# Hybrid pooling and gating layer on Trainium2: the first chunk's seven first weight units advance together, one block of h at a time

## The reference, cut to what matters

```python
mod = jax.nn.silu(c) @ w_ada + b_ada
shift, scale, gate = jnp.split(mod, 3, axis=-1)
h = _layer_norm(x) * (1 + scale[:, None]) + shift[:, None]
proj = h @ w_in                                  # 1024 -> 5 x 512
xa, ga, u, v, gb = jnp.split(proj, SPLITS, axis=-1)
ya = _pool_mixer(xa, w_pool, pool_scale) * jax.nn.silu(ga)
yb = _sgu_mixer(gelu(u), gelu(v), sgu_ln_g, sgu_ln_b, w_sgu, b_sgu) * jax.nn.silu(gb)
y = jnp.concatenate([ya, yb], axis=-1) @ w_out
z = DEEPNORM_ALPHA * x + gate[:, None] * y
return _layer_norm(z) * ln_g + ln_b
```

## Time and profile before

| | |
|---|---|
| median of 3 runs | 708.24 us (707.89 to 710.29) |
| span of the profiled execution | 708.7 us |
| TensorE busy | 684.2 us (97%), 3141 matmuls |
| VectorE busy | 531.2 us (75%) |
| ScalarE busy | 258.0 us (36%) |
| GpSimd busy | 108.3 us (15%) |
| HBM read | 89.94 MB |

### The profile page before, as it was taken

The page is one execution under the profiler, slowest core; times in us unless marked ns, Lnnn a source line. Parts: engine busy times, 40 slices in busy tenths (PEclk is TensorE's granted clock), DMA queues, the critical chain, the costliest instruction groups (busy, mean ns, idle before and its releaser), DMA issues.

```text
span 708.7 us, 8888 instructions
## 1 busy us (share of the span) xinstructions
PE 684.2 (97%) x3141; PEld 569.3 (80%) x3141; DVE 531.2 (75%) x942; ACT 258.0 (36%) x344; POOL 108.3 (15%) x96
## 2 busy tenths in 40 slices
PE   8789999899999999999999999999999999999993
PEld 8668888778888888888888888888888888888882
DVE  5876778995559979886468988886476997656387
ACT  4426435436412343334521243334621344332201
POOL 2461115520002201000002210110001210000005
PEclk9689999999999999999999999999999999999997
DMA  8933574216232561334233453234222532225203
GB/s 343 344 130 118 181 291 154 90 59 238 90 114 95 177 231 68 118 115 154 90 119 111 140 211 131 89 119 178 89 96 83 178 121 101 100 79 220 95 1 118
DMA packets 28362, 98.81 MB, mean 139 GB/s; under 512 B 3074, under 2 KB 4130, under 8 KB 28324
## 3 DMA queue, kind: packets, MB, share of 16 engines
q1 hardware_dynamic: 28324, 98.34, 39.2%
HBM read 89.94 MB, written 8.39 MB: 139 GB/s over the span
## 4 chain that ended last, share of the span: by engine, by line
PE 81%; DVE 13%; POOL 2%; issue 2%; ACT 1%; DMA 1%; SPq 0%; DVEq 0%; ACTq 0%; POOLq 0%
PE bank_b L852 51%; PE bank_a L852 25%; DVE v_gelu L571 4%; PE bank_b L876 2%; PE bank_a L945 1%; DVE w_low L533 1%; DMA x_norm<-in_x 1%; POOL gate_rows L359 1%; PE bank_b L902 1%; DVE sum_b L652 1%; DVE x_stats L552 1%; DVE z L732 1%; DVE z_stats L734 1%; DVE x_norm L558 1%; DVE tanh L729 1%
## 5 line engine op out<-in xcount | busy, mean ns | idle before, releaser
L852 PE MATMUL bank_b<-h_high,w_high 128*128 128x512 f32 x512 | 201.0, 393 | 0.0
L852 PE MATMUL bank_b<-h_high,w_low 128*128 128x512 f32 x512 | 199.4, 389 | 0.0
L852 PE MATMUL bank_b<-h_low,w_high 128*128 128x512 f32 x512 | 199.3, 389 | 0.0
L533 DVE TENSOR_TENSOR w_low<-w_float,w_high 128x1024 fp32r<-128x1024 f32 x108 | 137.0, 1269 | 48.6 <-ACT w_high L415 48.6
L415 ACT ACTIVATE w_high<-w_float 128x1024 fp32r<-128x1024 f32 x112 | 118.3, 1057 | 135.2 <-PE bank_a L852 61.0
L852 PEld LDWEIGHTS bank_b<-h_high,w_low 128*128 128x128 f32 x512 | 96.1, 188 | 20.3
L852 PEld LDWEIGHTS bank_b<-h_high,w_high 128*128 128x128 f32 x512 | 96.1, 188 | 19.9 <-issue 0.2
L852 PEld LDWEIGHTS bank_b<-h_low,w_high 128*128 128x128 f32 x512 | 96.2, 188 | 19.8 <-issue 0.2
L322 POOL TENSOR_TENSOR z_rstd<-z_var_eps,minus_half 128x1 f32<-128x1 f32 x16 | 21.6, 1351 | 359.9 <-DVE z_var_eps L737 359.9
L852 PE MATMUL bank_a<-w_high,h_high 128*128 128x512 f32 x128 | 52.7, 412 | 0.0
L852 PE MATMUL bank_a<-w_low,h_high 128*128 128x512 f32 x128 | 51.8, 405 | 0.0
(11 more groups left out here) (142 smaller groups left out, 975.7 us busy)
## 6 DMA issues: line engine op xcount, KB each, us to landing
w_float<-in_w_units SPq DMA_DIRECT2D x112, 512.0 KB, 3.3
z<-in_mod_units SPq DMA_DIRECT2D x20, 512.0 KB, 6.3
x_norm<-in_x SPq DMA_DIRECT2D x16, 512.0 KB, 5.3
z<-in_x SPq DMA_DIRECT2D x16, 512.0 KB, 4.2
out<-z SPq DMA_DIRECT2D x14, 512.0 KB, 4.7
ln_g_rows<-in_mod_units SPq DMA_DIRECT2D x2, 512.0 KB, 8.4
ln_b_rows<-in_mod_units SPq DMA_DIRECT2D x2, 512.0 KB, 8.8
out<-z SPq DMA_DIRECT2D x4, 256.0 KB, 2.0
```

What stands on the lines that cost most here:

```text
L533: vec.tensor_tensor(wL[:, n % S_SLOTS, :], wF[:, n % F_SLOTS, :], wH[:, n % S_SLOTS, :].bitcast(F32), ALU.subtract).then_inc(w_low, 1)
L852: last = mm(bank, wl if n == 2 else wh, ml if n == 1 else mh, start=start and n == 0, stop=stop and n == 2)
```

## The change

It touches the first chunk only, but for three added waits.

- SyncE loads all four x tiles first, and then eight weight units in the order EARLY = (0, 4, 5, 6, 1, 2, 3, 7), each after two mods.
- A mod of the first four serves one block of h instead of two (the host packs them so). TensorE multiplies mods 0 to 4 itself, VectorE adds up the other 11.
- Whole x tiles are turned (eight transposes each) into two banks, and ScalarE (tiles 0 and 1) and VectorE (tiles 2 and 3) copy the turned, normalised x back over its tile in x_norm. `h_evacuate` reads it from there. The last x tile is normalised by VectorE. The short warm-ups after the first 22 are gone.
- TensorE takes each block k of h through the v unit, unit 4 and unit 5, and, after each second block, unit 6. These use A, B0, B1 and B2; B3 keeps the shift and scale columns.
- GpSimd makes no subtraction any more; it computes the offsets of x. VectorE makes all low halves. Unit 6 borrows the buffers v_high and v_low.
- The parts of the gating matrix and its bias are prepared before the gelu of v in ScalarE's program, and pool and gating products come after units 8 and 9 instead of 7 and 8, and 11 instead of 10.

```diff
+POOL_AFTER_FIRST = (8, 11, 14, 18)
+SGU_AFTER_FIRST = (9, 11, 14, 18)
+EARLY = (0, 4, 5, 6, 1, 2, 3, 7)
+EARLY_CHANNEL = (4, 5, 6)
-PE_MODS = (0, 1)
+PE_MODS = (0, 1, 2, 3, 4)
-WARM_UP = (22, 1, 3, 0, 4)
+WARM_UP = 22
...
+            for p, unit in enumerate(EARLY):
+                for m in range(2 * p, 2 * p + 2):
+                    load_m(m)
+                load_w(0, p, unit)
...
                 if isinstance(c, int) and c == 0:
+                    act.wait_ge(staged_act, 2)
+                    act.wait_ge(staged_dve, 2)
+                    act.wait_ge(mod_ready, (1, 2)[k] if k < 2 else 2 + k // 2)
...
+                    nc.scalar.activation(hH[:, k, :].rearrange("p (j t) -> p j t", j=TILES), staged(k), ACT.Identity,
+                                         bias=shift, scale=scale).then_inc(h_high, 1)
...
+            small_weights()
+            sgu_bias()
+
             def chunk(c, first, last):
...
+                            wait(act, gb_gated, c * G + g)
                             nc.scalar.activation(tanh[:, :], B[:, 1, :], ACT.Tanh, scale=0.5).then_inc(ga_tanh, 1)
...
-                    if (n + AHEAD < UNITS or not last) and not (first and n + AHEAD < V_UNITS):
+                    if (n + AHEAD < UNITS or not last) and not (first and n + AHEAD < len(EARLY)):
                         split_low(c, n + AHEAD)
...
+            x_norm_of(0, TILES - 1, x0_last)
+            x_stage(2, B[:, 0:2, :])
+            mod_cols_of(0)
+            x_stage(3, A[:, 0:2, :])
+            split_low(0, 0, EARLY[0])
+            h_split(0, 0)
+            split_low(0, 1, EARLY[1])
+            split_low(0, 2, EARLY[2])
+            mod_cols_of(1)
+            mod_sum(5)
+            h_split(0, 1)
...
+            warm(WARM_UP)
+            turn_tile(0, A[:, 0:2, :])
+            turn_tile(1, A[:, 2:4, :])
+            mod_own_tile(0)
+            turn_tile(2, B[:, 0:2, :])
+            mod_own_tile(1)
+            pe.wait_ge(staged_act, 1)
+            turn_tile(3, A[:, 0:2, :])
+            pe.wait_ge(mod_ready, 1)
+            mod_own_tile(2)
...
+            for k in range(KT):
+                q = k // 2
+                pe.wait_ge(h_high, k + 1)
+                pe.wait_ge(w_low, EARLY.index(q) + 1)
+                early_v(k, (0, 1))
+                if k == 0:
+                    mod_own_tile(3)
+                pe.wait_ge(h_low, k + 1)
+                done = early_v(k, (2,))
+                if k % 2 == 1:
+                    done.then_inc(unit_done, 1)
+                if k == 1:
+                    pe.wait_ge(mod_ready, 2)
+                    mod_own(4)
+                if k == KT - 2:
+                    turn_w_sgu()
+                if k < KT - 1:
+                    early_channel(4, (k,))
+                    early_channel(5, (k,))
+                    if k % 2 == 1:
+                        early_channel(6, (k - 1, k))
+                        if q < V_UNITS - 1:
+                            mod_columns(q + 1)
+                else:
+                    sgu_bias()
+                    early_channel(4, (k,)).then_inc(unit_done, 1)
+                    early_channel(5, (k,)).then_inc(unit_done, 1)
+                    early_channel(6, (k - 1, k)).then_inc(unit_done, 1)
```

More of the change, by code:

```diff
@@ L205, in run_chunks, with after, w_slot, staged @@
             chunk(CHUNKS - 1, False, True)
+        def after(first):
+            return (POOL_AFTER_FIRST, SGU_AFTER_FIRST) if first else (POOL_AFTER, SGU_AFTER)
+        def w_slot(c, n):
+            early = isinstance(c, int) and c == 0 and n in EARLY
+            s = EARLY_SLOT[n] if early else n % S_SLOTS
+            if s == SPARE_SLOT:
+                return tuple(t[:, 0:2, :].rearrange("p a b -> p (a b)") for t in (vH, vL))
+            return wH[:, s, :], wL[:, s, :]
+        def staged(k):
+            return xn[:, :, k * P:(k + 1) * P]
         def m_sem(m):
@@ L752, in chunk @@
                     x_steps.begin(c + 1)
-                for n in range(UNITS):
-                    if (n + AHEAD < UNITS or not last) and not (first and n + AHEAD < V_UNITS):
+                if first:
+                    small_weights()
+                pool_after, sgu_after = after(first)
+                for n in range(V_UNITS if first else 0, UNITS):
+                    if (n + AHEAD < UNITS or not last) and not (first and n + AHEAD < len(EARLY)):
                         split_low(c, n + AHEAD)
@@ L773, in chunk @@
                             pooled_low(c, g)
+                            wait(dve, yp_ready, c * G + g)
                             gate(ga_tanh, ga_gated, sga, 1, c * G + g + 1)
@@ L889, in mod_own, with mod_own_tile @@
+            def mod_own_tile(m):
                 pe.wait_ge(c_ready, 1)
                 m_wait(pe, m)
-                for k in (2 * m, 2 * m + 1):
+                k_out = m // 2
+                for a in range(4):
+                    k = 4 * (m % 2) + a
+                    for i in range(2):
+                        col, at = a * 2 * P + i * P, 2 * i + k_out
+                        last = mm(B[:, 3, at:at + 1], m_slot(m)[:, col:col + P], csilu[:, k:k + 1],
+                                  start=(m % 2 == 0 and a == 0 and i == 0), stop=(m % 2 == 1 and a == 3),
+                                  skip_group_check=True)
+                last.then_inc(mod_multiplied, 1)
```

344 lines of the change are left out of this document (182 added, 162 removed).

## The result

The changed kernel takes **730.63 us** (median of 4 runs, 729.92 to 731.21), against 708.86 us for the kernel before (4 runs, 707.89 to 710.29) in the same session: a ratio of **1.031, interval 1.028 to 1.033**. It is slower, as forecast, but by some 22 us, where the forecast was 5.6 on the span. 730.6 lies outside the range of 707.6 to 720.2.

The account below looks back on a forecast made before the run. TensorE was taken to bound the seven first units, then VectorE the pooling: 90.6 + 9.4 + 0.75 + 61.8 = 162.6 against 156.97, so 708.7 + 5.6 = 714.3 span, median 713.8. Range 707.6 to 720.2.

Parts of the forecast that it names:

- The start: Up to block 1: first product about 19.9 us, half clock to about 28.6, block 1 at 31.4.
- From block 1 to the last v product: Seven-unit block on TensorE: products, sums, transposes and three waits of 1.0 take 39.3 us, ending at 70.7.
- rival 2: Clock keeps falling: two stretches at the start give +8.7 us, one more fall within the block +12; chance 0.22.
- From V to pooling 1: After the last v product: unit 8 starts 19.9 us later, TensorE stands 8.4, pooling of group 1 follows after 9.4.
- From pooling 1 on: VectorE sets the pace from pooling of group 1 to the fourth pool product: 61.8 us, plus 0.75.
- Nothing after it changes: Work behind the fourth pool product keeps the same units and weights, so no time is added there.
- The y of pool 0: This step now follows pooling and adds 0.75 us before the fourth pool product.
- The prediction's own sign: VectorE's stretch from pooling 1 to pool product 4 far from 62.5 us would show the forecast wrong.
- Costed at nothing: Added waits on gb_gated, yp_ready and ys_ready cost nothing; uncovered, one 0.7 operation a group.
- The median: Runs' median taken to lie 0.5 us below the profiled span, so 713.8 from a span of 714.3.
- Theory B: Experiments' theory: the loss is TensorE's own, the same 8 us at unit 8 and third pool product; cures come back.

Follow-up runs that it names:

- Experiment 4: Column sums of shift and scale moved ahead of the products of units 4 and 5, against the changed kernel: 723.44 us, ratio 1.020.
- Experiments 2 and 8: Against the changed kernel: 2, first x_rstd ahead of gate sum 3, 721.87 us; 8, gate sums 5 to 7 held for the pooled low half, 725.66 us.
- Warm start: Nine warm-up products added among the first transposes and shift-and-scale units, against the changed kernel: 725.63 us, ratio 1.023 to the kernel before.
- five mends: Changed kernel plus later bias copy, earlier x_rstd, earlier splits of units 8 to 10, covered column sums and nine warm-ups: 710.95 us, ratio 1.003.
- before and hold: Kernel before the change, with GpSimd's gate sums 5 to 7 held until the pooled low half of group 2 is made: 706.96 us, ratio 0.9976.
- four mends: Changed kernel plus later bias copy, earlier x_rstd, earlier splits of units 8 to 10 and covered column sums, no added warm-ups: 710.13 us, ratio 1.001.

## Why the prediction was wrong in size

**The start, right.** First product 20.48 (forecast about 19.9, and 20 to 23.5 in the last part); half clock to 32.5 (forecast 28.6 for its end); block 1 begins near 31.9 by the chain of waits (forecast 31.4). That the sum met it was in part luck: the clock fell at 18.8, not at 15.5 as before, and came back at 32.6 instead of 28.6, and the 3.3 us later and the 4.0 us later nearly cancel (13.8 us at half clock, 13.1 forecast). The copies from PSUM to x_norm took 1.23 and 1.22 on VectorE and 1.01 on ScalarE; 1.2 was taken. VectorE's timeline:

```profile
15.36 1.23 DVE L674 COPY x_norm<-bank_b 128x1024 f32<-128x1024 f32 x1 [2.06 <-PE bank_b L974]
...
17.97 1.22 DVE L674 COPY x_norm<-bank_a 128x1024 f32<-128x1024 f32 x1 [0.77 <-PE bank_a L974]
```

**From block 1 to the last v product, the first step that failed.** "TensorE needs VectorE's column (0.2) and ScalarE's first h_high (0.7): 3 x 1.0 of waiting. Together 39.3" put V at 70.7; it came at 77.6. The waits were there, three times, and 1.18 to 1.25 long: 0.7 more in all. What was left out is the clock behind them, 5.1 (the 1.1 that is left of the 6.9 is the start's 0.5 and small gaps). That is rival 2, which had one more fall in the block, at 3.3 us, and a chance of 0.22; there were three, at 1.7 us each. I discounted it by the one wait at 39.63 that left the clock alone, and that wait was 0.27 long, a fourth of these. Experiment 4 shows it: without the waits, 47 us at 1.00 and V at 69.5. The Trainium skill ("TensorE: Matmul & The Clock Gate", "A second HAM failure mode: psum-queue depth-cycling") describes short idle times between groups of products that make the clock swing and lists the price as re-throttling; this trace agrees as far as that goes, with 1.2 us of idle time and then 3.4 us at half clock, three times over. The page's case is another, a kernel that cycles through PSUM banks.

**From V to pooling 1, right.** Unit 8 started at V + 20.0 behind a hole of 8.35 (forecast 19.9 and 8.4), and the clock stood at 0.50 behind it. Pooling 1 came 10.3 after unit 8 (forecast 9.4): 0.9 off, as a weight load that was issued at 101.12 was rounded only from 105.66.

**From pooling 1 on, the second step that failed.** "Nothing after it changes: same units, same weights" and "The y of pool 0 ... adds 0.75" made this stretch 36.8 + 0.75 up to the third pool product; it was 43.1. The reasoning looked at the amount of work, and the work was the same. What had changed was the phase: GpSimd's and ScalarE's side chains (scaled z tile, gate sum, x_rstd) hang on loads and units, VectorE's main chain on pooling, and the two now met otherwise. Idle time of VectorE in the stretch rose by 3.8 (2.9 of it before x_norm, 3.35 against 0.45), collisions with gate sums by 1.9, and the foreseen 0.75 came on top: 6.5 against the 6.3 measured. Experiments 2 and 8 took 4.7 and 3.7 out of it separately, and both together brought it to 34.8. The prediction's own sign was "VectorE's stretch from pooling 1 to pool product 4 is far from 62.5": it was 68.6 (107.89 to 176.53). And the fourth pool product came at 176.53, not "near 163, still waiting for VectorE": it waited for nothing, since TensorE was now the later of the two.

**The rest, 1.7 us more.** From the third to the fourth pool product it is 0.5 more (25.6 against 25.0): half clock behind the 10.2 us wait, from 151 to 155.4, is some 2.2 us lost, and the 1.34 that the fourth product waited before is gone. Behind the fourth product it is 1.2 more (553.0 against 551.7), and TensorE has one wait there that it did not have before, 1.17 us at 398.51, put down to "issue". Warm start, five mends and before and hold have no such wait, and their stretch behind the fourth product is 551.6 to 551.7; in six others it is 0.4 to 0.7 long, and the stretch 552.4 to 552.7. What holds TensorE there is open; no run isolates it.

**Costed at nothing, rightly.** The added waits of the reordered y and gate steps end no wait of TensorE in the list above, and the x tiles came as computed: the statistics of the fourth began at 9.94 without a wait (forecast 9.9).

**The median.** 713.8 took the runs' median to lie 0.5 below the profiled span, and here it lies 1.1 above it (730.63 and 729.5; each run's time is some 1.7 above its own span, as 731.21 with 729.5). That is 1.6 us of the 16.8 by which the median was off.

**Theory B fell.** The wait at unit 8 and the wait at the third pool product were cured one by one, and their gains added.

## What to carry to other kernels

When a block of work is reordered, write the program order of every engine behind it, the small side chains included, and ask of each operation in that order whether its input now comes later than its neighbours'. Two one-line changes of order (a bias copy ahead of a gelu, a gate sum ahead of an rstd) cost 4.9 and 4.7 us here; the first stood in the diff, the second was an unchanged line that had become wrong. Treat an uncovered hand-over of 1.2 us in TensorE's stream as costing more than itself: in the changed kernel the three cost nearly 3 each, clock and all, and moving one column sum behind products of another unit removed it. And before crediting a gain of a few us in the median to an edit, cut the span into legs between marks in each trace, and take from each its time at half clock: here the clock at the start alone moved V by 5 us in programs that are equal up to there.

## What the chip did that I had not expected

- **Short waits can cost the clock at once.** Three waits of 1.18, 1.25 and 1.25 us in a stream that was otherwise busy at 1.00 were followed by about 3.4 us at 0.50 each, in which TensorE was fully busy. The seven kernels that have these three waits show 21 of them; 16 were followed by some 3.4 us at 0.50, which began between the end of the wait and some 1.6 us later, and five were not. In the kernel with GpSimd's subtractions put back, for one, the first two (at 39.9 and 51.8) were followed by none. In the four kernels with covered sums the clock fell, apart from the start, only once ahead of V, right behind the one wait of 1.09 us there; waits of 0.61 and 0.21 us were followed by no fall. And in the kernel with four mends the clock fell for 3 us at 72.8 with no wait before it, behind the small bias products. So a wait of this length is neither enough for a fall nor needed for one, but the V of 69.5 with covered sums against 77.6 shows what three can cost.
- **The length of the half-clock stretch at the start varies between executions and variants** that have the same TensorE program there: it ended at 32.5, 31.4, 26.0 and 23.5 us in four of them, after 13.8, 13.6, 10.4 and 3.4 us, and V moved with it (77.6, 76.7, 72.7, 72.6; the third of these also has two falls fewer in the block, worth 3.4). No run shows whether the execution, the session or the build decides it. Warm-up products moved its beginning from 18.9 to 23.1 and its end to 33.4.
- **A gate sum on GpSimd holds one VectorE operation until it is done.** A split of 1.22 became 2.53, a subtraction of 0.68 became 2.83, an x_norm of 0.81 became 2.88; they ended 1.1, 0.55 and 0.55 us behind the gate sum they met, as if most of their work came after it. A VectorE operation that reads PSUM beside it kept its 0.68 (gate_a at 129.92 in the kernel with four mends, under a gate sum that ran to 132.25). The Trainium skill ("GPSIMD Engine Reference", "1. Specifications") says the SBUF interfaces are shared with VectorE when it has two SBUF inputs or is in a 2-port mode; these rows agree.
